# Index keys turned through four banks, new keys turned amid later blocks, finer waits, and another opening with the sample rows as 128 rows of 128

## The chip, the cores and the metric

The kernel runs on one core of one Trainium2 chip. The metric is the device time of one execution in microseconds (us), as the median of several executions. TensorE is called PE, VectorE DVE, ScalarE ACT, GpSimd POOL (Pool) and SyncE SP. "The profiled execution" is one more execution, recorded by the hardware profiler.

## The reference, cut to what matters

One decoder layer for 512 prompt tokens and 8 sample tokens (one per sequence), all in float32, `D_MODEL` 2048:

```python
h = x * rsqrt(mean(x*x) + 1e-6) * g            # RMSNorm of 512 + 8 rows
z = h @ w_in                                   # 2048 x 8848, columns split into
# q_r k_r v_r g_r | q_a k_a v_a g_a | q_i (16 heads x 128) k_i (128) w_i (16)
# retention: chunks of 128 tokens, per-head norm, gate silu(g_r)
# sparse attention: score = sum_h w_i * relu(q_i . k_i); top 128 of the prompt,
#   top 256 of 4097 for a sample (its 4096 old index keys lie in pages of
#   cache_kidx); softmax over the chosen keys; gate silu(g_a)
x = x + concat(ret, att) @ w_out
y = rmsnorm(x, final_norm_g)
```

Outputs are `y`, the new keys, values and index keys, and the retention states.

## The kernel before, in words

Each engine runs its own instruction list, written out in order by hand; semaphores join them. `X.wait_ge(s, n)` holds engine X until semaphore s has reached n, and everything behind it on that engine waits too.

**Blocks of the projection.** The weights are taken in 43 blocks of 256 columns (`chunk(n, a)`: block n, half a of the 2048 rows). SP loads a half into `Wraw` (`weights`), ACT copies it to a rounded high part `Wh` (`hi`), Pool subtracts to get the low part `Wl` (`lo`), and PE multiplies three times (Wh x Hh, Wh x Hl, Wl x Hh: lines 1448 to 1450) into PSUM banks 0 to 3. ACT empties the banks (`evacuate`, counted by `acc_free`). Block 0 is the index keys and index weights alone, blocks 1 to 8 the index queries (`q_i`), 9 and 10 the new keys and values (`kaT`, `vaT`), 11 to 18 attention queries and gates, 19 to 34 the retention heads (two blocks a head, h = (n - 19) / 2), 35 to 42 the output projection.

**The opening.** Five x tiles arrive in the order 0, 1, samples, 2, 3 (`ARRIVAL`). The sample tile has 8 rows of 2048. ACT takes the sums of squares (`squares`), DVE the inverse root (`norms`, `rsqrt`: two integer operations and three Newton steps of three operations) and scales the rows by it and by the gain (`scale`, L1016), PE turns each tile in four groups through banks 4 to 7 (`turn_tokens`), ACT copies a group to `Hh` (`high`), DVE subtracts to `Hl` (`low`, L1025). Then PE multiplies block 0 (`index_keys`, `index_weights`). `keep_busy` is turns of the identity whose result nobody reads.

**The index scores.** After block 8, PE makes 48 products `q_i . k_i` in banks 4 to 7, ACT takes relu into banks 1 and 2 in turn, DVE adds them up with the weights (L1083, `si_acc`) into `bm`.

**The old index keys.** Pool gathers 32 tiles `kx` of 512 KB into nine buffers (L870). PE turns them in 64 steps u (`turn_keys(u)`, four turns each) through three banks (3, 4, 5, by u % 3), ACT copies each step to one of six slots of `kT` (`keys_out(u)`, L650), and after every four steps, a group G, PE makes four products with the sample queries (`products(G)`, L1587), ACT a relu (`relu_group`, L658), and every second group PE two row products (`row_product`, L1596). Turn u waits for copy u - 3; copy u (from 6 on) waits for `products((u - 6) // 4)`. The first copy waits until DVE has added all 48 (`si_acc`), because of an `act.wait_ge(si_acc, n_si)`.

**The new keys and values** are turned (20 turns) after block 10 and copied to `kan` and `van` for storing and for attention.

**Retention head h = HP = 2.** Pool issues 16 small indirect DMAs (`candidate_rows`, `rowf`, L894), eight ahead of `rotary(h, 0)` and eight behind `rotary(h, 1)`; between the two lies `lo(n + 1, 1)`, the low part for block 24's second half.

**Before the output projection** DVE does `stats(7)` (the last head's norm), `keep_states_out(7)`, `samples_low` (low part of the sample columns, counted by `ms_lo`), `mix_low`, and the norm of the sample outputs (`gs_n`). PE's block 35 needs `ms_lo` for its third part and `gs_n` ahead of its second half.

Of the kernel before, what the change touches and what calls it, by code (L numbers as in the profile page):

```python
# [37 lines left out]
P = 128  # L38
# [39 lines left out]
def build(nc, x_prompt, x_sample, cache_k, cache_v, cache_kidx, state_ret, page_table, norm_g, w_in,  # L78
# [3 lines left out]
    with ctx:  # L82
# [56 lines left out]
        ptb, o = place("ptb", [P, NS, PAGES], I32, o)  # L139
        scores, o = place("scores", [NS * SEC, SKEY + 4], F32, 0)  # L140
# [13 lines left out]
        kT = mix[:, 0:6, 0:T]  # L154
# [68 lines left out]
        def turned_tile(v, r):  # L223

            return bank[4 + v % 4][:, :].rearrange("p (k t) -> p k t", k=4)[:, :, 0:r]
# [3 lines left out]
        x_in = [sem(f"x_in{i}") for i in range(5)]  # L229
        x_sq = sem("x_sq"); st4_set = sem("st4_set"); g_tr = sem("g_tr"); g_row = sem("gain_row_in"); ones_set = sem("ones_set"); g_mm = sem("gain_rows_mm"); x_norm = sem("x_norm"); x_tr = sem("x_tr")  # L230
# [32 lines left out]

        wiv = w_in[0].rearrange("(k p) c -> p k c", p=P)
# [74 lines left out]
        def _(sp):  # L339
# [30 lines left out]
            sp.wait_ge(x_in[2], 16)  # L370
            weights(0, 0)
            weights(0, 1)
# [98 lines left out]
        def _(act):  # L471
# [93 lines left out]
            def squares(i, c):  # L565

                act.wait_ge(x_in[i], 16)
                r = rows(i)
                if i == QT:
                    act.wait_ge(st4_set, 1)  # L570
                if c:
                    act.wait_ge(x_sq, c)
                nc.scalar.activation(junk[0:r, :], XT[0:r, i, :], ACT.Square,
                                     accum_out=st4[0:r, c:c + 1]).then_inc(x_sq, 1)

            def high(pos, which=range(4)):

                i = ARRIVAL[pos]
                for g in which:
                    v = 4 * pos + g  # L580
                    act.wait_ge(x_tr, v + 1)
                    nc.scalar.activation(Hh[:, 4 * g:4 * g + 4, tok(i)], turned_tile(v, rows(i)),
                                         ACT.Copy).then_inc(h_hi, 1)

            for pos, i in enumerate(ARRIVAL):
                src = x_prompt[0, P * i:P * i + P, :] if i < QT else x_sample.rearrange("b o m -> (b o) m")
                act.dma_start(XT[0:rows(i), i, :], src).then_inc(x_in[i], 16)
            act.dma_start(ptb[:, :, :].rearrange("p b j -> p (b j)"),
                          page_table.rearrange("b j -> (b j)").partition_broadcast(P)).then_inc(s_ptab, 16)
            for c, i in enumerate(ARRIVAL):  # L590
                squares(i, c)
# [3 lines left out]
            high(1)  # L595
            high(2)
            high(3)
            high(4)
# [28 lines left out]
            for t in range(1, QT):  # L627
                for h in range(NIH):
                    w = P * (t + 1)
                    act.wait_ge(si_mm, i + 1)  # L630
                    if i >= 2:
                        act.wait_ge(si_acc, i - 1)
                    nc.scalar.activation(bank[1 + i % 2][:, 0:w], bank[4 + i % 4][:, 0:w], ACT.Relu).then_inc(si_relu, 1)
                    i += 1
            n_si = i
# [8 lines left out]
            act.wait_ge(si_acc, n_si)  # L644

            def keys_out(u):
                act.wait_ge(kx_tr, u + 1)
                if u >= 6:
                    act.wait_ge(kq_mm, (u - 6) // 4 + 1)
                nc.scalar.activation(kT[:, u % 6, :], bank[3 + u % 3][:, :], ACT.Copy).then_inc(kt_ev, 1)  # L650
# [30 lines left out]
            for n in (9, 10):  # L681
                hi(n + 1, 0)
                if n == 9:
                    act.wait_ge(sc_out, 3)
                evacuate(n)
                hi(n + 1, 1)
            for m in range(4):
                dst = kan if m < 2 else van
                c = slice(P * (m % 2), P * (m % 2) + P)
                act.wait_ge(kv_tr, 2 * m + 1)  # L690
                nc.scalar.activation(dst[:, 0:QT, c], bank[4 + m % 2][:, :].rearrange("p (t d) -> p t d", t=QT),
                                     ACT.Copy).then_inc(kv_ev, 1)
                act.wait_ge(kv_tr, 2 * m + 2)
                nc.scalar.activation(dst[0:NS, QT, c], bank[6 + m % 2][0:NS, 0:P], ACT.Copy).then_inc(kv_ev, 1)
# [20 lines left out]
            for n in range(11, 19):  # L715
                hi(n + 1, 0)
                attention(2 * n)
# [119 lines left out]
        def _(pool):  # L837
# [12 lines left out]

            pool.wait_ge(g_mm, 4)
# [69 lines left out]
            for h in range(NH):  # L921
# [54 lines left out]
        def _(dve):  # L976
# [10 lines left out]
            def rsqrt(x, done=None):  # L987
# [3 lines left out]
                link(v_.tensor_scalar(y.bitcast(I32), x.bitcast(I32), 1, None, ALU.arith_shift_right))  # L991
                link(v_.tensor_scalar(y.bitcast(I32), y.bitcast(I32), -1.0, float(0x5f3759df), ALU.mult, ALU.add))
# [10 lines left out]
            def norms(a, b):  # L1003

                s = st4[:, a:b]
                dve.wait_ge(x_sq, b)
                link(v_.tensor_scalar(s, s, 1.0 / DM, EPS, ALU.mult, ALU.add))
                rsqrt(s)

            def column(i):  # L1010

# [924 lines left out]
```

## Time and profile before

| | |
|---|---|
| median of 3 runs | 1217.83 us (1217.45 to 1219.92) |
| the profiled execution: its time / its span | 1220.82 us / 1219.0 us |
| PE busy | 1176.8 us, 97% of the span |
| DVE, ACT, POOL busy | 51%, 37%, 47% |
| mean granted TensorE clock | 0.99 |
| chain that ended last | PE 91%, DVE 4%, ACT 2%, DMA 1% |

The span is from the first to the last instruction; 1.8 us lie around it. Busy time of an engine is a mean over stages, so with PE at 97% the question for each stage is where its 42 us without work lie and which engine ended each of those waits.

### The profile page before, as it was taken

How to read it: one execution, taken by the hardware profiler on the slowest of the kernel's cores; microseconds unless marked ns; L12 is line 12 of the kernel's file. 1: busy time of each engine (PE TensorE's matmuls, PEld its weight loads, DVE VectorE, ACT ScalarE, POOL GpSimd, SP SyncE). 2: the span in 40 equal slices, each digit the busy share in tenths (PEclk: the TensorE clock that was granted, in tenths of full speed). 3: DMA queues.
4: the chain of work that ended last, by engine and by line, in shares of the span. 5: the costliest groups of instructions: out<-in, count | busy, mean ns of one | idle time of the engine just before them, and what ended most of it. 6: DMA issues, size and time to landing. Idle time of an engine off the chain costs nothing.

```text
span 1219.0 us, 21955 instructions
## 1 busy us (share of the span) xinstructions
PE 1176.8 (97%) x9172; PEld 1110.3 (91%) x9172; DVE 620.0 (51%) x1199; ACT 452.1 (37%) x791; POOL 570.6 (47%) x262
## 2 busy tenths in 40 slices
PE   7999999899999999999999989999999999999995
PEld 5999995456999999999999979999999999999995
DVE  6500005998996994899998305343442544010013
ACT  5322225664223333333424323342524253232332
POOL 1355545240434333333635485846666384546450
PEclk9999999999999999999999999999999999999998
DMA  7233346380242222222343316446353525432213
GB/s 271 77 113 118 123 126 235 116 266 17 75 134 70 70 84 93 70 70 70 87 113 99 107 35 176 113 116 165 101 154 88 141 70 200 134 103 78 94 35 140
DMA packets 152840, 138.58 MB, mean 114 GB/s; under 512 B 4653, under 2 KB 145053, under 8 KB 151069
## 3 DMA queue, kind: packets, MB, share of 16 engines
q1 hardware_dynamic: 144502, 110.72, 30.5%
q0 software_dynamic: 6976, 22.03, 5.5%
q10 hardware_dynamic: 1280, 4.66, 1.0%
q8 instruction: 61, 1.00, 0.3%
q14 instruction: 21, 0.17, 0.0%
HBM read 127.02 MB, written 10.34 MB: 113 GB/s over the span
## 4 chain that ended last, share of the span: by engine, by line
PE 91%; DVE 4%; ACT 2%; issue 1%; DMA 1%; another core or an unknown queue 1%; DVEq 0%; ACTq 0%
PE bank L1448 25%; PE bank L1449 25%; PE bank L1450 25%; PE bank L1466 6%; PE bank L1559 2%; PE bank L1670 1%; PE bank L1652 1%; DVE bm L1083 1%; PE bank L1587 1%; DVE XT L1016 1%; PE bank L1825 1%; ACT mix L650 1%; DMA XT<-in_x_prompt 1%; PE bank L1596 1%
## 5 line engine op out<-in xcount | busy, mean ns | idle before, releaser
L1448 PE MATMUL bank<-Hh,Wh 128*128 128x264 f32 (+2 forms) x2432 | 711.8, 293 | 2.7 <-DVE Hl L1288 2.1
L1449 PE MATMUL bank<-Hl,Wh 128*128 128x264 f32 (+2 forms) x2432 | 703.4, 289 | 0.4 <-issue 0.4
L1450 PE MATMUL bank<-Hh,Wl 128*128 128x264 f32 (+2 forms) x2432 | 702.2, 289 | 0.5 <-issue 0.4
L842 POOL TENSOR_TENSOR Wl<-Wraw,Wh 128x2048 fp32r<-128x2048 f32 x84 | 386.8, 4606 | 477.3 <-ACT Wh L489 476.9
L1448 PEld LDWEIGHTS bank<-Hh,Wh 128*128 128x128 f32 x2432 | 459.7, 189 | 7.3 <-issue 6.4
L1449 PEld LDWEIGHTS bank<-Hl,Wh 128*128 128x128 f32 x2432 | 459.6, 189 | 3.1 <-issue 2.7
L1450 PEld LDWEIGHTS bank<-Hh,Wl 128*128 128x128 f32 x2432 | 458.7, 189 | 1.5 <-issue 1.5
L489 ACT ACTIVATE Wh<-Wraw 128x2048 fp32r<-128x2048 f32 x84 | 160.5, 1912 | 362.5 <-PE bank L1450 362.3
L1387 DVE TENSOR_TENSOR Y<-Y,bank 128x512 f32 (+1 forms) x16 | 10.4, 685 | 163.1 <-PE bank L1466 163.1
L1066 DVE COPY QS<-mix 128x128 f32<-128x128 f32 x1 | 0.3, 281 | 140.4 <-ACT mix L495 140.4
L870 POOL DMA_INDIRECT kx<-in_cache_kidx,pidx x32 | 30.4, 950 | 45.2 <-PE bank L1466 38.0
L1466 PEld LDWEIGHTS bank<-ident,kx 128*128 128x128 f32 x256 | 27.1, 141 | 23.8 <-issue 21.1
L900 POOL TENSOR_TENSOR XS<-XS,rot 128x520 f32<-128x520 f32 x16 | 21.2, 1322 | 44.6 <-ACT XW L547 44.6
L1466 PE MATMUL bank<-ident,kx 128*128 128x128 f32 x256 | 34.9, 279 | 7.0 <-ACT mix L650 4.7
L650 ACT ACTIVATE mix<-bank 128x512 f32<-128x512 f32 x64 | 34.9, 609 | 18.0 <-PE bank L1587 10.1
L1113 DVE MAX8 best<-scores 32x8 f32<-32x1025 f32 x32 | 38.9, 1217 | 5.1 <-ACT scores L677 4.1
L1145 DVE MAX8 top<-cand 8x8 f32<-8x1024 f32 x32 | 38.9, 1215 | 1.0
L1115 DVE FIND_INDEX8 besti<-best,scores 32x8 uint32<-32x1025 f32 x32 | 38.6, 1207 | 0.0
L1147 DVE FIND_INDEX8 besti<-top,cand 8x8 uint32<-8x1024 f32 x32 | 38.6, 1205 | 0.0
L1149 DVE MATCH_REPLACE8 cand<-top,cand 8x1024 f32<-8x1024 f32 x32 | 38.3, 1197 | 0.0
L1117 DVE MATCH_REPLACE8 scores<-best,scores 32x1025 f32<-32x1025 f32 x31 | 37.2, 1199 | 0.0
L1559 PE MATMUL bank<-kiT,mix 128*128 128x256 f32 (+2 forms) x96 | 33.8, 504 | 2.2 <-issue 1.4
(258 smaller groups left out, 1226.9 us busy)
## 6 DMA issues: line engine op xcount, KB each, us to landing
Wraw<-in_w_in SPq DMA_DIRECT2D x36, 1024.0 KB
Wraw<-in_w_in SPq DMA_DIRECT2D x64, 512.0 KB
Wraw<-in_w_out SPq DMA_DIRECT2D x16, 1024.0 KB
XT<-in_x_prompt ACTq DMA_DIRECT2D x4, 1024.0 KB, 9.0
sp__98<-in_state_ret SPq DMA_DIRECT2D x8, 512.0 KB, 4.0
out<-sp__98 SPq DMA_DIRECT2D x8, 512.0 KB, 5.1
Y<-in_x_prompt SPq DMA_DIRECT2D x1, 4096.0 KB
out<-Y SPq DMA_DIRECT2D x4, 1024.0 KB
```

The lines of the kernel that those rows point to most:

```text
L489: nc.scalar.activation(Wh[:, a, :, :], Wraw[:, a, :, :], ACT.Copy).then_inc(w_hi, 1)
L650: nc.scalar.activation(kT[:, u % 6, :], bank[3 + u % 3][:, :], ACT.Copy).then_inc(kt_ev, 1)
L842: nc.gpsimd.tensor_tensor(Wl[:, a, :, :], Wraw[:, a, :, :], Wh[:, a, :, :].bitcast(F32), ALU.subtract).then_inc(w_lo, 1)
L1113: link(v_.max(top, row))
L1115: link(v_.max_index(besti[:, 8 * (k // 3):8 * (k // 3) + 8], top, row))
L1145: link(v_.max(top, cand[:, :]))
L1147: link(v_.max_index(besti[0:NS, 8 * (k // 3):8 * (k // 3) + 8], top, cand[:, :]))
L1448: mm(bank[i][:, 0:w], wh, Hh[:, kk, s], start=(a == 0 and k == 0), stop=False)
L1449: mm(bank[i][:, 0:w], wh, Hl[:, kk, s], start=False, stop=False)
L1450: last = mm(bank[i][:, 0:w], wl, Hh[:, kk, s], start=False, stop=(a == 1 and k == KC - 1))
L1466: return nc.tensor.transpose(out, in_, ident[0:k, 0:k])
L1559: mm(bank[4 + i % 4][:, 0:w], mix[:, h, tok(t)], kiT[:, 0:w], start=True, stop=True).then_inc(si_mm, 1)
```

## The change

Seven edits; the diff below is cut to their core.

1. The sample rows are loaded as 128 rows of 128 (row 8k + b is piece k of sample b), their squares summed by one matmul with a 0/1 matrix `same`, scaled with gains `gs0` of that shape, and turned in one step instead of 16.
2. The inverse roots of tiles 0 and 2 move from DVE to Pool (`norm_root`: 14 chained operations on one column); the two integer operations of DVE's `rsqrt` become one, everywhere. The loads change order: the first weights are issued by ACT between tile 2 and tile 3, the page table by SP. Tile 1 is turned through banks 0 to 3. The fillers are 16 and 8 turns with the `same` matmul between them and 8 behind tile 0; the 8 ahead of `index_keys` go. `index_weights` of the first half stands ahead of tile 3's turns.
3. The index scores start at `acc_free` 32, with finer waits for the last two heads.
4. Old index keys: four banks (3, 4, 5, 2) and eight slots; the first turns wait for their own bank, the first copies for `qs_ready`.
5. The new keys are turned after the first half of block 10, the new values after the first half of block 11.
6. Two of the second eight `candidate_rows` move ahead of `lo(n + 1, 1)`.
7. `samples_low` stands ahead of `stats(7)`.

```diff
+        KB = (3, 4, 5, 2)
+        TURN_BANK = (4, 5, 6, 7, 0, 1, 2, 3, 4, 5, 6, 7, 4, 5, 6, 7, 4)
 # SP
+            sp.dma_start(gs0[:, :], ...to_broadcast([KT, NS, P])).then_inc(gs_in, 16)
-            sp.wait_ge(x_in[2], 16)
-            weights(0, 0)
-            weights(0, 1)
+            sp.wait_ge(x_in[3], 16)
+            sp.dma_start(ptb...)
 # ACT, opening
-            for c, i in enumerate(ARRIVAL): squares(i, c)
-            high(0) hi(0, 0) hi(0, 1) high(1) high(2) high(3) high(4)
+            rows_in(0) rows_in(1)  xs0 <- x_sample  rows_in(2)
+            first_weights(0) first_weights(1) rows_in(3)
+            squares(0, 0) squares(1, 1) squares(QT, 2) squares(2, 3)
+            high(0) hi(0, 0) hi(0, 1) high(1) high(QT) squares(3, 4) high(2) high(3)
 # ACT, keys
-            act.wait_ge(si_acc, n_si)
+            act.wait_ge(qs_ready, 1)
             def keys_out(u):
                 act.wait_ge(kx_tr, u + 1)
-                if u >= 6:
-                    act.wait_ge(kq_mm, (u - 6) // 4 + 1)
-                nc.scalar.activation(kT[:, u % 6, :], bank[3 + u % 3][:, :], ...)
+                if u >= 8:
+                    act.wait_ge(kq_mm, (u - 8) // 4 + 1)
+                nc.scalar.activation(kT[:, u % 8, :], bank[KB[u % 4]][:, :], ...)
 # Pool
+            def norm_root(a, b):      # every operation waits for the one before
+                link(g_.tensor_scalar(x, x, 1.0 / DM, EPS, ALU.mult, ALU.add))
+                link(g_.tensor_scalar(y..., x..., -0.5, float(0x5f3759df), ...))
+                for step in range(3):
+                    link(tensor_tensor) link(tensor_tensor) link(tensor_scalar)
+                    ins = g_.tensor_tensor(y if step < 2 else x, z, y, ALU.mult)
+            pool.wait_ge(x_sq, 1)
+            norm_root(0, 1)
+            pool.wait_ge(x_sq, 4)
+            norm_root(3, 4)
             pool.wait_ge(g_mm, 4)      # then the low parts of block 0
@@
                 rotary(h, 0)
+                if h == HP:
+                    candidate_rows(range(NS, NS + 2))
                 lo(n + 1, 1)
                 rotary(h, 1)
                 if h == HP:
-                    candidate_rows(range(NS, 2 * NS))
+                    candidate_rows(range(NS + 2, 2 * NS))
 # DVE
-                link(v_.tensor_scalar(y, x, 1, None, ALU.arith_shift_right))
-                link(v_.tensor_scalar(y, y, -1.0, float(0x5f3759df), ...))
+                link(v_.tensor_scalar(y, x, -0.5, float(0x5f3759df), ...))
-            norms(0, 2) scale(0) scale(1) norms(2, 5) low(0) low(1) scale(QT)
-            scale(2) low(2) scale(3) low(3) low(4)
+            (after the gb copies) scale(0, 1)          # waits rstd 1, from Pool
+            (mean of tile 1; wait sum_mm; mean of samples) rsqrt(st4[:, 1:3])
+            scale(1, 0) scale(QT, 0) low(0) low(1) low(QT)
+            scale(2, 2) rsqrt(st4[:, 4:5]) scale(3, 0) low(2) low(3)
@@
+            samples_low(KC, 1)
             stats(NH - 1)
             keep_states_out(NH - 1)
-            samples_low(KC, 1)
 # PE, opening
-            keep_busy(24, 6)
-            turn_tokens(0)
-            turn_tokens(1)
-            keep_busy(8, 3)
+            keep_busy(16, 6)
+            (wait x_sq 3, gb_copied 4) mm(bank[3][:, 0:1], same, xs2[:, 0:1])
+            keep_busy(8, 6)
+            turn_tokens(0, 1)
+            keep_busy(8, 2)
+            turn_tokens(1, 2)
+            turn_tokens(QT, 3)
             pe.wait_ge(h_lo, 8)
             pe.wait_ge(w_lo, 1)
             index_keys(0, slice(0, CUT))
-            turn_tokens(2)
-            turn_tokens(3)
+            turn_tokens(2, 4)
             pe.wait_ge(w_lo, 2)
             index_keys(1, slice(0, CUT)).then_inc(acc_done, 1)
-            turn_tokens(4)
             index_weights(slice(P, CUT))
-            pe.wait_ge(h_lo, 20)
+            turn_tokens(3, 5)
+            pe.wait_ge(h_lo, 17)
 # PE, scores and keys
-            pe.wait_ge(acc_free, 36)
+            pe.wait_ge(acc_free, 32)
+                    if t == 1 and h >= NIH - 2:
+                        pe.wait_ge(acc_free, 36 - 2 * (NIH - 1 - h))
-            pe.wait_ge(si_relu, i)
-            pe.wait_ge(qs_ready, 1)
-                if u >= 3:
-                    pe.wait_ge(kt_ev, u - 2)
+                if u >= 4:
+                    pe.wait_ge(kt_ev, u - 3)
+                elif u == 3:
+                    pe.wait_ge(si_acc, i)
+                elif u:
+                    pe.wait_ge(si_relu, i - 4 + u)
-            pe.wait_ge(si_acc, i)          # behind the first four turns
+            pe.wait_ge(qs_ready, 1)
+            pe.wait_ge(si_relu, i)
 # PE, new keys and values
             chunk(10, 0)
+            turn_new(0)                    # waits acc_free 40
             chunk(10, 1)
-            pe.wait_ge(acc_free, 44)
-            (all 20 turns)
+            chunk(11, 0), turn_new(1)      # waits acc_free 44
```

ACT's copies of the new keys and values follow in the same way: `new_out(0)` behind `hi(11, 0)`, `new_out(1)` behind `hi(12, 0)`.

## Rows read from the trace of the kernel before

**Rows 1.** Waits of PE over the whole span: waiter <- releaser, us, times, longest

```profile
PE bank L1466 <- ACT mix L650: 4.7, 11, 0.7
PE bank L1466 <- DVE Hl L1025: 3.9, 2, 3.4
PE bank L1825 <- ACT vn L781: 3.6, 1, 3.6
...
PE bank L1466 <- ACT bank L633: 1.3, 1, 1.3
PE bank L1466 <- ACT kan L694: 1.1, 1, 1.1
...
PE bank L1466 <- ACT vaT L532: 0.5, 1, 0.5
```

**Rows 2.** Timeline of DVE in the opening: start, duration, instruction

```profile
11.66 0.17 DVE L991 TENSOR_SCALAR rsq<-st 128x2 int32<-128x2 int32 x1
...
13.83 4.62 DVE L1016 SCALAR_TENSOR_TENSOR XT<-XT,st,gb 128x2048 f32<-128x2048 f32 x2
...
20.73 3.28 DVE L1025 TENSOR_TENSOR Hl<-bank,Hh 128x512 fp32r<-128x512 f32 x5
...
37.10 2.48 DVE L1025 TENSOR_TENSOR Hl<-bank,Hh 128x512 fp32r<-128x512 f32 x4 [1.11 <-ACT Hh L582]
```

**Rows 3.** Timeline of PE in the opening

```profile
21.57 3.50 PE L1466 MATMUL bank<-ident,XT 128*128 128x128 f32 x16 [3.37 <-DVE Hl L1025]
...
26.49 0.38 PE L1504 MATMUL bank<-Hh,W0h 128*128 128x256 f32 x1 [0.55 <-DVE Hl L1025]
...
35.83 1.91 PE L1466 MATMUL bank<-ident,XT 128*128 128x128 f32 x16
```

**Rows 4.** PE by stretches: stretch, us, busy (instructions), granted clock, DMA share, GB/s

```profile
22.00:23.00 1.00, 1.00 (x7) 0.50 0.00 0
...
1015.00:1016.00 1.00, 1.00 (x6) 0.50 1.04 313
```

**Rows 5.** Groups of instructions on POOL, shapes apart: count, busy us, mean ns

```profile
L918 POOL TENSOR_TENSOR QZ<-XS,XW 128x8 f32<-128x8 f32 x8 | 1.7, 212 | 0.0
```

**Rows 6.** Timeline of PE in the stage of the old index keys

```profile
226.88 1.53 PE L1466 MATMUL bank<-ident,kx 128*128 128x128 f32 x12 [1.29 <-ACT bank L633]
...
230.66 1.07 PE L1587 MATMUL bank<-mix,QS 128*32 128x512 f32 x8
...
288.14 1.07 PE L1587 MATMUL bank<-mix,QS 128*32 128x512 f32 x8 [0.69 <-ACT mix L650]
```

**Rows 7.** Timeline of ACT in the same stage

```profile
227.89 3.05 ACT L650 ACTIVATE mix<-bank 128x512 f32<-128x512 f32 x6 [0.94 <-DVE bm L1083]
...
251.06 1.58 ACT L650 ACTIVATE mix<-bank 128x512 f32<-128x512 f32 x3 [1.51 <-PE bank L1466]
```

**Rows 8.** Stretch 228 to 292 of all engines: busy of PE, PEld, DVE, ACT, POOL first

```profile
228.00:292.00 64.00, 57.28 (x431) 31.45 (x430) 58.80 (x151) 42.65 (x82) 21.77 (x23) 1.00 0.57 190
```

**Rows 9.** Stretch 230 to 277 of PE, in which Pool gathers

```profile
230.00:277.00 47.00, 41.95 (x311) 1.00 0.77 258
```

**Rows 10.** Timeline of DVE where attention first needs it

```profile
377.74 1.02 DVE L1171 SCALAR_TENSOR_TENSOR pb<-bank,bm 128x512 f32<-128x512 f32 x2 [10.90 <-PE bank L1652]
```

**Rows 11.** Timeline of POOL in head h = 2

```profile
707.62 4.61 POOL L842 TENSOR_TENSOR Wl<-Wraw,Wh 128x2048 fp32r<-128x2048 f32 x1
...
726.78 4.54 POOL L842 TENSOR_TENSOR Wl<-Wraw,Wh 128x2048 fp32r<-128x2048 f32 x1
```

**Rows 12.** Timeline of PE in head h = 2, last turn ahead of block 24's second half

```profile
712.03 0.27 PE L1466 MATMUL bank<-ident,pads 128*72 128x128 f32 x1
```

**Rows 13.** Timeline of PE in block 35

```profile
1014.63 0.54 PE L1448 MATMUL bank<-Hh,Wh 128*128 128x264 f32 x1 [2.10 <-DVE Hl L1288]
...
1022.50 0.27 PE L1466 MATMUL bank<-ident,OSn 128*128 128x128 f32 x1
```

**Rows 14.** Timeline of DVE in block 35

```profile
1020.86 0.35 DVE L1367 TENSOR_SCALAR OSn<-OSn,mv,st 128x128 f32<-128x128 f32 x1
```

More of the change, by code:

```diff
@@ L585, in _ @@
[L585 to L591, printed above, removed]
+                if i == QT:
+                    nc.scalar.activation(junk[:, 0:P], xs0[:, :], ACT.Square, accum_out=xs2[:, 0:1]).then_inc(x_sq, 1)
+                else:
+                    nc.scalar.activation(junk[:, :], XT[:, i, :], ACT.Square,
+                                         accum_out=st4[:, c:c + 1]).then_inc(x_sq, 1)
@@ L592, in _ @@
+            rows_in(0)
+            rows_in(1)
+            act.dma_start(xs0[:, :], x_sample[:, 0, :].rearrange("b (k c) -> k b c", k=KT)).then_inc(x_in[QT], 16)
+            rows_in(2)
+            first_weights(0)
+            first_weights(1)
+            rows_in(3)
+            squares(0, 0)
+            squares(1, 1)
+            squares(QT, 2)
+            squares(2, 3)
             high(0)
@@ L595, in _ @@
             high(1)
+            high(QT)
+            squares(3, 4)
             high(2)
             high(3)
-            high(4)
             hi(1, 0)
@@ L678, in _, with new_out @@
                                  bias=cols[0:NS * SEC, 6, 0:1]).then_inc(sc_out, 1)
[L681 to L694, printed above, removed]
+            def new_out(which):
+                for m in (2 * which, 2 * which + 1):
+                    dst = (kan, van)[which]
+                    c = slice(P * (m % 2), P * (m % 2) + P)
+                    act.wait_ge(kv_tr, 2 * m + 1)
+                    nc.scalar.activation(dst[:, 0:QT, c], bank[4 + m % 2][:, :].rearrange("p (t d) -> p t d", t=QT),
+                                         ACT.Copy).then_inc(kv_ev, 1)
+                    act.wait_ge(kv_tr, 2 * m + 2)
+                    nc.scalar.activation(dst[0:NS, QT, c], bank[6 + m % 2][0:NS, 0:P], ACT.Copy).then_inc(kv_ev, 1)
+            hi(10, 0)
+            act.wait_ge(sc_out, 3)
+            evacuate(9)
+            hi(10, 1)
+            hi(11, 0)
+            new_out(0)
+            evacuate(10)
+            hi(11, 1)
             def exps(h):
@@ L1628, in _, with turn_new @@
             chunk(9, 1)
+            def turn_new(which):
+                pe.wait_ge(acc_free, 40 + 4 * which)
+                for m in (2 * which, 2 * which + 1):
+                    src = (kaT, vaT)[which][:, m % 2, :]
+                    if m >= 2:
+                        pe.wait_ge(kv_ev, 2 * m - 2)
+                    for t in range(QT):
+                        last = turn(bank[4 + m % 2][:, P * t:P * t + P], src[:, tok(t)])
+                    last.then_inc(kv_tr, 1)
+                    turn(bank[6 + m % 2][0:NS, 0:P], src[:, T:NT]).then_inc(kv_tr, 1)
             chunk(10, 0)
+            turn_new(0)
             chunk(10, 1)
[L1632 to L1640 removed]
             def query_key(h):
@@ L1676, in _ @@
                     chunk(n, a)
+                    if n == 11 and a == 0:
+                        turn_new(1)
                     beta = 2 * n + a
```

159 lines of the change are left out of this document (95 added, 64 removed).

## The prediction

> **What bounds the kernel now.** I read the page first: PE is busy for 97% of the span, so a change can save only PE's work, PE's waits, or the slow clock that follows a wait. This change removes almost no PE work. I therefore read PE's list of waits next, because each entry names a place and a releaser. The reader should see three kinds in it [rows 1]: waits in the ring of the old index keys (4.7 us on ACT's copies, L650, and 1.3 at its start, L633), single waits at handovers (3.9 in the opening, 3.6 in head 2, 1.1 and 0.5 at the new keys), and one of 2.1 in block 35 [rows 13]. The timeline of each place then tells what would be late next, and the stretches tell the granted clock there.
>
> After two of these waits PE ran at 0.50 of its clock, 1.2 GHz: in the opening after 3.37 us without work, and in block 35 after 2.1 us [rows 3, 4, 13]. So such a wait costs more than itself. For the price I take block 35's matmuls: 0.22 us apart at the low level and 0.12 at the high one, over 3.4 us, which is about 1.6 us lost.
>
> **The opening (edits 1 and 2).** The old order of DVE is roots, two scalings, roots, and then eight subtractions of 0.656 us, which let PE's `index_keys` start at 26.49 [rows 2, 3]. In the new order:
> - The small identity sums and the four gain copies go ahead of everything. The identity is in SBUF at about 9 us, so the copies end near 12.1 instead of 10.9.
> - Pool's first root starts when tile 0's squares are there, at about 7.9. A Pool operation on 8 columns takes 0.212 us [rows 5]; with 0.08 for the link I take 0.29, and 14 of them end at 12.0. The lower bound is 0.21 each, and the upper is open, because this trace has no chained small Pool operations.
> - So DVE scales tile 0 from 12.1 to 14.4. It then does two means and ten root operations at 0.2 (one is 0.17 with a gap of 0.03 [rows 2]), 2.4 us, to 16.8; tile 1 to 19.1; the samples 0.3 to 19.4; and eight subtractions, 5.25 us, to 24.7. `index_keys` starts at about 24.8, which is 1.7 us earlier. Pool's low parts of block 0, behind two roots, are ready by 22.
>
> PE then loses most of this gain. Between the sample turn (about 21.3) and 24.8 it has no work for 3.5 us, and the 8 fillers that stood there are gone. The row for the same length of wait shows the clock at 0.50 right behind it [rows 3, 4], so 24 matmuls at first go 0.22 apart, about 1.5 us lost. From 26.3 in warm time: `index_keys` to 29.3, tile 2's turns 2.0, `index_keys` 2.9, `index_weights` 1.9, so tile 3's turns start at 36.1 against 35.83 before. Before, the weights' 1.9 us covered the copies and subtractions of the last tile; now nothing does. From the start of the turns to the last subtraction is 3.75 us (35.83 to 37.10 + 2.48) [rows 2, 3], giving 39.85 against 39.58. From there PE alone sets the pace, and block 1's weights are there 3 us ahead. I count the opening as 0. The bounds are 1.5 us saved (clock stays high) and 2.5 us lost (slower Pool steps).
>
> The Trainium skill speaks against this edit (TensorE: Matmul & The Clock Gate, What's actually happening): "the default state is throttled, and activity releases the throttle", so taking fillers out of a pause costs. The trace agrees, with 0.50 after the pause of 3.37 us. By the rule alone the opening would be slower; by the rows it is even, since DVE arrives earlier.
>
> **The start of the scores (edit 3).** PE may start 0.8 us earlier, but ACT's first relu stands behind `hi(9, 1)`, and after it DVE's additions, 0.855 us apart at the end, set the pace. Worth nothing, neither way.
>
> **The old index keys (edit 4).** First the start. The first copy waited for the last addition, at 227.89 [rows 7]; PE started turning at 226.88. Now u = 0, 1, 2 are turned from 225.6, ACT copies from 227.0, and only u = 3 (bank 2) waits for the last addition. Four turns of 0.51 from 228.0 give `products(0)` at 230.05 instead of 230.66 [rows 6]: 0.6 us.
>
> Then the ring. From `products(0)` to `products(15)` it takes 57.5 us [rows 6], 7.66 for two groups. PE's work for two groups is 8 turns of 0.51 (12 instructions in 1.53), two products of 1.0 and two row products of 0.42, in all 6.9. Over 7.5 pairs that leaves 5.7 us; the stretch shows 6.7 us without PE work from 228 to 292 [rows 8]. The waits follow from the order of ACT: turn u needs copy u - 3, and copy 4G + 6 needs `products(G)`, so twice a pair PE stands for 0.35 to 0.7 us. With four banks and eight slots, copy 4G + 6 needs only `products(G - 1)`, and a turn's bank was copied three turns (1.5 us) before; those waits go. What stays is a late ACT: four times in this stage it starts 0.8 to 1.8 us late while Pool issues gathers [rows 7], and a fourth bank covers about half of such a delay. I take 4.7 of the 6 us. Bounds: 2.4 (half of the waits come back) and 6.2 (all gone). Together with the start: 5.3 us, between 3 and 7.
>
> What is late next? The gathers must deliver 2.1 MB in 6.9 us, 304 GB/s; they ran at 258 with a DMA share of 0.77 [rows 9], which scales to 335. Close, but enough. DVE is still choosing from `bm` until 290.3, so it gains nothing from scores that come at 289; it had 10.9 us of slack where attention first needs it [rows 10], and loses about 4 of that.
>
> **The new keys (edit 5).** PE's waits of 0.5 and 1.1 [rows 1] vanish: both sets of turns now have copies behind them that ended a half block earlier. The 20 turns stay. ACT's 3.4 us of copies fall into half blocks of 12 us in which it has over 5 us free, and SP's stores are reached before the weights behind them are due. 1.6 us, with bounds of 1.2 and 1.8.
>
> **Head 2 (edit 6).** Pool has no gap from 693.8 to 731.3, so moving two issues (2.5 us) does not shorten it. It does delay the low part that began at 707.62 by 2.5 us, to end at 714.7, and PE reaches block 24's second half at 712.3 [rows 11, 12]. So a new wait of 2.4 us appears there, with the low clock behind it (1.6). In exchange the old wait of 3.6 on `vn` [rows 1], which ended 1.4 us after Pool's last issue, shrinks, since Pool's last issue stays at 726.8 and PE gets there later. Block 25 needs the low part that ends at 731.3 [rows 11]; PE got there at 732.0. Net 0, with bounds of 1.5 either way.
>
> **Block 35 (edit 7).** `samples_low` now runs in DVE's idle 2 us ahead of `stats(7)`, so PE's wait of 2.1 us and the low clock behind it go, 3.7 us. But next PE waits for `gs_n`. Its turn stood at 1022.5; the DVE result it needs was there at 1021.15 [rows 13, 14] and comes only 0.45 us earlier (two root operations, one subtraction). PE arrives at about 1019.0 and waits 1.7 us. The turn comes at 1020.8: 1.7 us saved, 0.1 if this pause lowers the clock again, 2.5 at best.
>
> **The tail.** One root operation less on the last chain: 0.2 us.
>
> **Sum.** 0 + 0 + 5.3 + 1.6 + 0 + 1.7 + 0.2 = 8.8 us. The profiled execution took 1220.82 us, 1219.0 of it span; that makes 1212.0. It is 3.0 above the median of 1217.83 shown, so for the median I predict 1209.0 us.
>
> **The rivals.**
> - *The ring is bound elsewhere* (14%). If late copies or the gathers keep PE waiting, edit 4 gives 1 to 2 us instead of 5.3. For it: DMA share 0.77 already, and ACT's late starts. Against it: no PE wait in the list names a DMA. Time: about 1213.
> - *The clock decides* (10%). PE's new pauses (before `index_keys`, block 24, `gs_n`) each bring the low level and nothing is given back: -1.5, -1.6 and -1.6 against my terms, about 1213.5. The reverse (the clock holds everywhere, and the whole ring becomes PE's own pace) gives about 1205 (15%).
> - *Slower* (5%): Pool's chained roots. If one step costs x instead of 0.29 us, tile 0 is scaled 14(x - 0.29) later and the whole opening follows. To eat 8.8 us, x must be 0.92 us; slower by more than 0.2% starts at 1.09. At 1.2 us the time is 1221.6. Against it: the 0.212 us row [rows 5]. The Trainium skill names the reason why Pool's small operations are dear (GPSIMD Engine Reference, 3.1 Elementwise): two software hops for each instruction and a join of eight cores.
> - *The moves do nothing measurable* (5%): gains before 300 us are taken back where DVE's choosing or Pool's chain in head 2 is the clock of the kernel. About 1217. Against it: DVE's 10.9 us of slack, and head 2 follows PE's own turns.
>
> **How the numbers follow.** My own case has 51% and lies within 1206 to 1212. I hold 0.2%, 2.4 us, to be about what a measurement of this kernel can tell from no change. The range takes in the fast case, the ring and the clock: 1204.0 to 1214.5. Outside it lie the last two rivals and little more. Faster by over 0.2% (under 1215.4): 51 + 14 + 10 + 15, less 1 for their edges, and 0 of the last two, so 0.89. Within 0.2%: 0.07. Slower: 0.04.
>
> **What the profile of the changed kernel would show.** Right: `index_keys` starts near 24.8 and the last subtraction of the opening ends near 39.8; `products(0)` to `products(15)` takes 51 to 54 us; no waits of PE on `kan` or `vaT`; a new wait on `Wl` (L842) near 704 of the new time; and PE waits on L1367 instead of L1288 in block 35. Wrong: Pool steps over 0.4 us apart, PE waiting for `kx` by DMA, or a low clock behind new pauses in which I count none.

## The result, and the profile after

| | before | after |
|---|---|---|
| median on the chip | 1217.94 us (12 runs) | 1222.95 us (12 runs, 1217.93 to 1224.76) |
| profiled execution: time / span | 1220.82 / 1219.0 us | 1223.86 / 1222.1 us |

The ratio is 1.0029, with an interval of 1.0018 to 1.0040: the change makes the kernel slower by 0.29%. (This ratio is estimated over the executions of both kernels and is not the quotient of the two medians, which is 1.0041 here; the same holds for the ratios further down.) I had predicted 1209.0 us, and slower had 4%.

The page of the changed kernel, its first part (busy us, share of the span, instructions):

```profile
PE 1173.9 (96%) x9159; PEld 1110.6 (91%) x9159; DVE 626.6 (51%) x1185; ACT 448.7 (37%) x788; POOL 580.1 (47%) x290
```

PE has 2.9 us less to do than before and 6 us more in which it does nothing. So the waits must tell it. PE's waits over the whole span, in the form of [rows 1]:

```profile
PE bank L1533 <- DVE kg L1330: 5.2, 1, 5.2
PE bank L1579 <- DVE Hl L1082: 4.9, 2, 3.0
PE bank L1566 <- issue: 4.3, 1, 4.3
...
PE bank L1515 <- POOL Wl L879: 2.8, 1, 2.8
PE bank L1913 <- DVE vx L1394: 2.1, 1, 2.1
PE bank L1533 <- DVE OSn L1434: 2.0, 1, 2.0
PE bank L1533 <- DVE XT L1075: 1.7, 2, 1.3
PE bank L1533 <- ACT mix L680: 1.5, 3, 0.5
```

What the change was to remove is gone: the ring's 4.7 is 1.5, and no wait names `kan` or `vaT`. In their place stand single long ones that were not there: 4.3 at the sum matmul of the samples (L1566), 5.2 and 2.1 behind DVE in head 2. The next step is to cut both timelines at matmuls that both have. The lengths between them, in us:

| from the landmark before to | before | after | difference | predicted |
|---|---|---|---|---|
| first matmul of the scores | 190.17 | 195.60 | +5.4 | 0 |
| `products(0)` | 40.49 | 39.74 | -0.75 | -0.6 |
| `products(15)` | 57.48 | 52.45 | -5.0 | -4.7 |
| first attention matmul on `kaT` | 88.46 | 86.33 | -2.1 | -1.6 |
| head 1, first matmul of `vn` with `kn` | 293.63 | 293.64 | 0 | 0 |
| head 3, the same | 115.46 | 121.04 | +5.6 | 0 |
| head 7, the same | 217.27 | 217.24 | 0 | 0 |
| the end | 216.04 | 216.06 | 0 | -1.9 |

They add up to the spans, 1219.0 and 1222.1. Three terms came as forecast or a little better. Two places that I had counted at zero cost 11 us, and the last term, block 35, brought nothing. Each length is that of one profile. The first has a spread: with the same opening as in the changed kernel the scores start at 194.18 (e3), 194.67 (e4) and 195.60, so the loss there is 4 to 5.4 us.

**The opening.** ACT in the changed kernel; `ACTq` rows are its own DMA issues:

```profile
2.37 0.67 ACTq L603 DMA_DIRECT2D XT<-in_x_prompt  x1
3.06 4.03 ACTq L607 DMA_DIRECT2D Wraw<-in_w_in  x2
7.12 4.87 ACTq L603 DMA_DIRECT2D XT<-in_x_prompt  x1
12.02 1.28 ACT L592 ACT_TABLE_LOAD   x1 [12.02 <-issue]
13.31 1.91 ACT L592 ACTIVATE junk<-XT 128x2048 f32<-128x2048 f32 x1
```

An issue of one block of rows takes 0.67 us at first. The two weight loads (each 128 x 8 pieces of 576 bytes) take 4.03 us to issue, and the block of rows behind them 4.87. Only then is ACT free for the squares: 13.31, against 5.83 in the kernel before:

```profile
5.83 1.91 ACT L573 ACTIVATE junk<-XT 128x2048 f32<-128x2048 f32 x1 [0.78 <-DMA XT<-in_x_prompt]
```

DVE scales tile 0 at 19.29 (13.83 [rows 2]), and PE:

```profile
21.70 3.32 PE L1533 MATMUL bank<-ident,XT 128*128 128x128 f32 x16 [1.33 <-DVE XT L1075]
...
31.26 0.54 PE L1579 MATMUL bank<-Hh,W0h 128*128 128x256 f32 x1 [2.97 <-DVE Hl L1082]
```

`index_keys` starts at 31.26 where [rows 3] had 26.49. The low clock follows the pause, as forecast: the matmuls start 0.21 us apart (stretch, us, busy of the five engines, granted clock, DMA share, GB/s):

```profile
32.00:34.00 2.00, 2.00 (x12) 2.00 (x11) 2.00 (x1) 0.00 (x0) 2.00 (x2) 0.50 1.08 376
```

**Head 2.** DVE first, then Pool, in the same microseconds:

```profile
711.72 2.89 DVE L1388 TENSOR_TENSOR kst<-raws,kst 8x128 fp32r<-8x128 f32 x1 [14.15 <-ACT raws L800]
...
722.97 6.02 DVE L1394 TENSOR_TENSOR vx<-vst,eye 72x1024 fp32r<-72x1024 f32 x1
...
740.07 8.45 DVE L1330 COPY_PREDICATED kg<-isnew,nkb 128x256 f32<-128x256 int32 x4 [7.71 <-DMA kg<-in_cache_k,rowu]
```

```profile
707.39 4.55 POOL L879 TENSOR_TENSOR Wl<-Wraw,Wh 128x2048 fp32r<-128x2048 f32 x1
...
723.38 4.53 POOL L879 TENSOR_TENSOR Wl<-Wraw,Wh 128x2048 fp32r<-128x2048 f32 x1
...
738.33 4.57 POOL L879 TENSOR_TENSOR Wl<-Wraw,Wh 128x2048 fp32r<-128x2048 f32 x1
743.35 4.53 POOL L879 TENSOR_TENSOR Wl<-Wraw,Wh 128x2048 fp32r<-128x2048 f32 x1 [0.46 <-ACT Wh L508]
```

The same operations in the kernel before, DVE and then Pool:

```profile
723.47 1.22 DVE L1327 TENSOR_TENSOR vx<-vst,eye 72x1024 fp32r<-72x1024 f32 x1
...
741.73 4.21 DVE L1263 COPY_PREDICATED kg<-isnew,nkb 128x256 f32<-128x256 int32 x4 [7.70 <-DMA kg<-in_cache_k,rowu]
```

```profile
740.01 4.61 POOL L842 TENSOR_TENSOR Wl<-Wraw,Wh 128x2048 fp32r<-128x2048 f32 x1
746.88 4.59 POOL L842 TENSOR_TENSOR Wl<-Wraw,Wh 128x2048 fp32r<-128x2048 f32 x1 [2.27 <-ACT Wh L489]
```

Read the lists by their ends. In the changed kernel Pool's subtraction ends at 727.91 and `vx` at 728.99. Pool's next two end at 742.90 and 747.88, and the four copies into `kg` end at 748.5. In the kernel before `vx` took 1.22 us in all eight heads, and the copies met one subtraction only: it ended at 744.62 and they at 745.94, before the next one began. Each of these DVE operations stands until Pool's subtraction is over, and does its own work then. PE waits for both, and for the late `Wl` at 712.00 that the prediction had.

From head 1's landmark to head 3's PE stands for 12.0 us in the changed kernel and 5.2 in the kernel before, 6.8 more. In turn PE is busy for 1.2 us less (109.1 and 110.3), as the low clock lasts less: in the kernel before it was 0.50 from 728 to 734, behind the wait of 3.6 us on `vn`; in the changed kernel it was 1.00 behind the wait of 2.8 us and about 0.5 to 0.6 only from 748 to 752. That leaves the 5.6 us of the table.

### The profile page after: what moved, and what is told of

It reads as the page before. It is cut to its first block, busy times and chain, and to the rows that moved or that the text cites. A ratio compares the mean times of both kernels' runs of the same rounds, so it can differ in the third digit from the quotient of the medians.

```text
span 1222.1 us, 21941 instructions
## 1 busy us (share of the span) xinstructions
PE 1173.9 (96%) x9159; PEld 1110.6 (91%) x9159; DVE 626.6 (51%) x1185; ACT 448.7 (37%) x788; POOL 580.1 (47%) x290
## 4 chain that ended last, share of the span: by engine, by line
PE 87%; DVE 6%; POOL 2%; issue 2%; ACT 1%; ACTq 1%; DMA 0%; DVEq 0%; POOLq 0%
PE bank L1515 24%; PE bank L1516 24%; PE bank L1517 24%; PE bank L1533 6%; PE bank L1752 1%; PE bank L1734 1%; PE bank L1634 1%; DVE bm L1150 1%; PE bank L1664 1%; POOL rowf L957 1%; PE bank L1673 1%; DVE Hl L1082 1%; ACTq L603 1%; PE bank L1909 0%; DVE kg L1330 0%
## 5 line engine op out<-in xcount | busy, mean ns | idle before, releaser
L1533 PE MATMUL bank<-ident,kx 128*128 128x128 f32 x256 | 32.4, 277 | 2.3 <-ACT mix L680 1.5
```

The costliest lines, as they stand in the source:

```text
L1533: return nc.tensor.transpose(out, in_, ident[0:k, 0:k])
```

## The experiments

Ratios are to the kernel before on the same chip and in the same round, with their intervals. Rounds e and f ran on one chip and round g on another. The kernel before took 1218.68 us in round e and 1221.78 in round f, so between rounds ratios are compared, not medians.

| run | median us / before | ratio |
|---|---|---|
| e1 first weights issued by SP | 1214.75 / 1218.68 | 0.9966 (0.9951 to 0.9981) |
| e2 roots back on DVE | 1222.60 / 1218.68 | 1.0025 (1.0011 to 1.0038) |
| e3 candidate rows 8 and 8 | 1216.86 / 1218.68 | 0.9987 (0.9978 to 0.9996) |
| e4 Pool waits for `vx` | 1219.95 / 1218.68 | 1.0016 (1.0008 to 1.0025) |
| f1 e1 and e3 together | 1212.55 / 1221.78 | 0.9921 (0.9902 to 0.9940) |
| f2 f1, old order in block 35 | 1212.36 / 1221.78 | 0.9927 (0.9902 to 0.9952) |
| f3 kernel before with edit 4 alone | 1217.86 / 1221.78 | 0.9963 (0.9946 to 0.9980) |
| f4 e3, one load on ACT | 1215.10 / 1221.78 | 0.9941 (0.9920 to 0.9961) |
| g1 f2 with the old opening | 1210.46 / 1218.17 | 0.9940 (0.9925 to 0.9956) |
| g2 f1, the pause filled | 1209.18 / 1218.17 | 0.9929 (0.9915 to 0.9943) |
| g3 kernel before with edit 6 alone | 1224.99 / 1218.17 | 1.0042 (1.0026 to 1.0058) |
| g4 e1 and e4 together | 1212.15 / 1218.17 | 0.9947 (0.9929 to 0.9965) |

### The opening: e1, e2, f4

Theory A: ACT is held by its own issues. Theory B: Pool's chained roots are slow. (Theory C and its rival D, in the expectations of e3 and e4, concern head 2.)

```diff
 e1 (SP's queue; the same two lines are taken from ACT's)
+            sp.wait_ge(x_in[2], 16)
+            weights(0, 0)
+            weights(0, 1)
             sp.wait_ge(x_in[3], 16)
```

> The changed kernel with one thing undone: the first block's two weight loads are issued by SP behind x tile 2 again, not by ACT between tiles 2 and 3. Theory A (ACT is held by its own DMA issues: 4.03 and 4.87 us for the weights and the fourth tile, so its first square starts at 13.3 us instead of 5.8): ACT's issues are over before 4 us, the first square starts near 5.9, index_keys near 25 instead of 31.3, and the time falls by about 6 us, to about 0.999 of before. Theory B (Pool's two chained roots set the opening): the roots stay, so the time falls by under 2 us.

```profile
2.37 1.16 ACTq L606 DMA_DIRECT2D XT<-in_x_prompt  x2
3.55 1.28 ACT L595 ACT_TABLE_LOAD   x1 [3.55 <-issue]
5.79 1.91 ACT L595 ACTIVATE junk<-XT 128x2048 f32<-128x2048 f32 x1 [0.95 <-DMA XT<-in_x_prompt]
```

Without the weight loads the two last blocks of rows are issued in 1.16 us, and the squares start at 5.79. `index_keys` starts at 23.74, 7.5 us sooner than in the changed kernel and 2.8 sooner than in the kernel before. The scores start at 187.97, 7.6 sooner than after, and the rest of the kernel keeps that. The ratio, 0.9966, is lower than the 0.999 that I expected: Theory A holds, and the issues cost more than I had put on them.

```diff
 e2: Pool's norm_root(0, 1) and norm_root(3, 4) go; on DVE
-            scale(0, 1)
+            dve.wait_ge(x_sq, 1)
+            link(v_.tensor_scalar(st4[:, 0:1], st4[:, 0:1], 1.0 / DM, EPS, ALU.mult, ALU.add))
+            rsqrt(st4[:, 0:1])
+            scale(0, 0)
 ... (tile 2 in the same way, column 3)
```

> The changed kernel with the roots of tiles 0 and 2 taken back from Pool to DVE; ACT still issues the first weights. Theory A (ACT's issues): ACT's first square still starts at 13.3, and only the difference between a Pool root (4.1 us) and a DVE root (2.2 us) is gained, at most 2 us on index_keys' start. Theory B (Pool's roots): the opening shortens by 5 us or more, to about 1.000 of before.

```profile
17.14 2.35 DVE L1071 SCALAR_TENSOR_TENSOR XT<-XT,st,gb 128x2048 f32<-128x2048 f32 x1
```

Tile 0 is scaled 2.2 us sooner, and `index_keys` starts at 29.08, also 2.2 sooner. But the scores start at 195.38, as in the changed kernel (195.60), and the ratio is 1.0025 beside 1.0029. The clock took most of the gain back. The `index_keys` of the last tokens start 1.75 us sooner (44.29, 46.04 in the changed kernel), both behind a wait of 1.90 us on `Hl`; here the granted clock fell behind it, and there it did not. PE by stretches, e2 and then the changed kernel:

```profile
46.00:48.00 2.00, 2.00 (x11) 0.50 0.03 8
```

```profile
46.00:48.00 2.00, 1.96 (x16) 1.00 0.04 12
```

Theory B falls: it asked for 5 us or more. The roots cost at most about 2 us of the opening, and e1, which leaves them on Pool, gives back more than the 5.4.

```diff
 f4 (with candidate rows 8 and 8): ACT's queue
             first_weights(0)
-            first_weights(1)
 SP's queue
+            sp.wait_ge(x_in[2], 16)
+            weights(0, 1)
             sp.wait_ge(x_in[3], 16)
```

> Candidate rows 8 and 8 again, and of the two first weight loads one stays on ScalarE (ahead of the last block of rows) and the second is issued by SyncE behind the third block of rows. Theory: ScalarE is held by the issues in proportion to what stands in its queue, so about half of the 7.6 us of the opening comes back: first square near 9.5 us, ratio half way between the two runs, 0.996. Rival: the queue only holds the engine once it is full, and one load does not fill it: first square at 6 us, the time of the run with both mended. Second rival: one load is enough to fill it, first square near 13, ratio 0.9987 as with the split alone undone.

```profile
3.01 0.51 ACTq L609 DMA_DIRECT2D Wraw<-in_w_in  x1
3.55 3.52 ACTq L605 DMA_DIRECT2D XT<-in_x_prompt  x1
7.11 1.28 ACT L594 ACT_TABLE_LOAD   x1 [7.11 <-issue]
8.40 1.91 ACT L594 ACTIVATE junk<-XT 128x2048 f32<-128x2048 f32 x1
```

One weight load is issued in 0.51 us, and it is the issue behind it that takes 3.52. So ACT is free at 3.55 with no load, 7.11 with one and 12.02 with two: 3.6 us for the first, 4.9 for the second. The hold grows with what stands in the queue, as the theory had it (first square at 8.4, I had said 9.5). `index_keys` starts at 26.36, between 23.70 with none and 31.26 with two, and the ratio is 0.9941 where I had expected 0.996: more than half came back. What in the queue holds the issue, the number of pieces, their size or the rows of x still ahead of them, no run separates.

### Head 2: e3, e4, g3, g4

```diff
 e3
-                if h == HP:
-                    candidate_rows(range(NS, NS + 2))
                 lo(n + 1, 1)
                 rotary(h, 1)
                 if h == HP:
-                    candidate_rows(range(NS + 2, 2 * NS))
+                    candidate_rows(range(NS, 2 * NS))
```

> The changed kernel with the second eight candidate-row gathers together again behind rotary(h, 1). Theory C (two gathers fewer at the end let Pool's low part of block 25 start while DVE's vx operation runs; vx and the predicated copy then stand behind Pool's, 6.0 and 8.1 us instead of 1.2 and 3.2, and the low part of block 24's second half comes 2.5 us late): head 2 costs what it did before, vx takes 1.2 us, the wait of 2.8 us on Wl goes, and the time falls by about 5 us, to 1.000 of before. Rival D (head 2 lost its time because PE arrives there earlier than before, whatever the order): the time stays within 1.5 us of the changed kernel.

```profile
719.08 1.22 DVE L1392 TENSOR_TENSOR vx<-vst,eye 72x1024 fp32r<-72x1024 f32 x1
736.43 4.12 DVE L1328 COPY_PREDICATED kg<-isnew,nkb 128x256 f32<-128x256 int32 x4 [7.80 <-DMA kg<-in_cache_k,rowu]
```

`vx` is back at 1.22 us, and the copies, at 4.12, meet one subtraction, as in the kernel before. From head 1 to head 3 it takes 114.76 us, against 121.04 after and 115.46 before: the split is what costs.

```diff
 e4, ahead of Pool's low part of block 25 (and in g4, with e1's edit)
+                if h == HP + 1:
+                    pool.wait_ge(vx_ready, h)
                 lo(n, 0)
```

> The changed kernel with one wait added: Pool starts the low part of block 25 only when DVE's vx of head 2 is done. Theory C: vx takes 1.2 us instead of 6.0, PE's wait of 2.1 us on vx goes, though Pool is about 1 us later; the predicated copy may meet a low part still. Time 2 to 4 us less than the changed kernel. Rival D: a wait more can only cost, up to 1 us more.

```profile
721.43 1.22 DVE L1396 TENSOR_TENSOR vx<-vst,eye 72x1024 fp32r<-72x1024 f32 x1
```

Only Pool's start is moved, by a wait of 0.89 us, and `vx` falls from 6.02 to 1.22 us. That shows the mechanism for `vx`. In this profile the copies met one subtraction only (3.49 us), and the stretch took 113.73 us; but that execution took 1215.14 us, and the ten others 1218.79 to 1221.19. Against the changed kernel the guard alone brings 1.6 us by the ratios (1.0016 beside 1.0029, and the intervals overlap), where e3 brings 5.1.

```diff
 g3, in the kernel before (edit 6 alone)
                 rotary(h, 0)
+                if h == HP:
+                    candidate_rows(range(NS, NS + 2))
                 lo(n + 1, 1)
                 rotary(h, 1)
                 if h == HP:
-                    candidate_rows(range(NS, 2 * NS))
+                    candidate_rows(range(NS + 2, 2 * NS))
```

> The kernel before with edit 6 alone: the first two of the later candidate rows are fetched between the two parts of the rotation, the other six behind it. Theory: Pool's long subtractions shift, and VectorE's operations with two operands in SBUF (the copy into kg, vx) stand behind them, as in the changed kernel: the stretch from head 1's to head 3's first state matmul (670.23 to 785.69) grows from 115.5 to about 121 us, ratio 1.0046. Rival (the prediction's step): net 0, within 1.5 us, ratio 0.999 to 1.001. Second rival: the loss in the changed kernel came from where the gains in front had put the fetches, and here it is about half.

```profile
726.07 2.53 DVE L1325 TENSOR_TENSOR vst<-raws,vst 8x128 fp32r<-8x128 f32 x1 [10.96 <-ACT raws L778]
728.63 1.22 DVE L1329 TENSOR_TENSOR vx<-vst,eye 72x1024 fp32r<-72x1024 f32 x1
741.00 8.39 DVE L1265 COPY_PREDICATED kg<-isnew,nkb 128x256 f32<-128x256 int32 x4 [7.78 <-DMA kg<-in_cache_k,rowu]
```

Two issues moved by one place, in the kernel before, cost 0.42%: from head 1 to head 3 it takes 122.08 us. `vx` is clear here, but the small `vst` ahead of it stood beside the subtraction (2.53 us, 0.28 in the kernel before), and the copies into `kg` (8.39 us) met two. PE waits 5.2 us for the copies, 2.9 for `Wl` and 1.7 for a `vx` that starts late. The loss needs none of the other edits; the "about half" of my second rival falls.

> The changed kernel with the first weight loads on SyncE, the candidate rows as the change has them, and Pool waiting in head 2 for VectorE's vx before its low part of block 25. Theory: it keeps vx clear but not the copies into kg, so it stays behind the run with both parts mended (0.9921) by about 3 us in most executions: ratio 0.994 to 0.995. Rival: as the profile with this guard alone showed 113.7 us between head 1's and head 3's state matmuls against 116.7 with both mended, the split is worth keeping once guarded: ratio 0.990.

With e1's opening the guarded split comes to 0.9947, as expected of it, behind 0.9921 of f1; the intervals overlap.

### The ring, the two undone together, and block 35: f1, f2, f3

```diff
 f3, in the kernel before (ACT's copies, then PE's turns; the products read slot % 8)
-                if u >= 6:
-                    act.wait_ge(kq_mm, (u - 6) // 4 + 1)
+                if u >= 8:
+                    act.wait_ge(kq_mm, (u - 8) // 4 + 1)
...
-                if u >= 3:
-                    pe.wait_ge(kt_ev, u - 2)
+                if u >= 4:
+                    pe.wait_ge(kt_ev, u - 3)
+                elif u == 3:
+                    pe.wait_ge(si_acc, i)
```

> The kernel before with the four banks and eight key slots alone (turns of index keys through banks 3, 4, 5, 2; nothing else of the change). Theory: the key stage is 5.0 us shorter, as measured in the changed kernel (52.4 against 57.4 us), and nothing gives it back: span 1214.0, time near 1213.5, ratio 0.9959. Rival: the blocks behind take it back, since their fetches and Pool's work stand at other places against VectorE: ratio 0.998 or above.

`products(0)` to `products(15)` takes 52.96 us, and the first attention matmul comes at 371.59 instead of 376.60. Of that, 4.5 us are the ring (57.48 before) and 0.5 lie ahead of `products(0)`. The span is 5.1 us less (1213.9), and the ratio of 0.9963 says 4.5.

> The changed kernel with two of its parts undone: the two first weight loads are issued by SyncE behind the third block of token rows, as in the kernel before, and the candidate rows are fetched 8 and 8 again. Theory: the two losses are apart in time and add, 7.6 us in the opening (scores and key stage end at 279.56 in place of 287.79 in the profile with the loads on SyncE) and about 6 us in head 2. From the changed kernel's span of 1222.1 that is near 1208.7, a time near 1210.5, ratio to the kernel before 0.993 to 0.995. Rival: a gain in front is given back in head 2, because Pool and VectorE then meet elsewhere: ratio 0.996 to 0.998, no better than with the loads moved alone.

f1 is the changed kernel with the diffs of e1 and e3. The two losses add: by the ratios e1 brings 0.0063 and e3 0.0042, and f1 0.0108. The ratio of 0.9921 is a little better than expected: a version that beats both kernels. From head 1 to head 3 it takes 116.72 us.

```diff
 f2 = f1 with
-            samples_low(KC, 1)
             stats(NH - 1)
             keep_states_out(NH - 1)
+            samples_low(KC, 1)
```

> As the run with both parts mended, and the lower halves of the samples' mixture stand behind the last head's statistics again, as in the kernel before (edit 7 undone). Theory: in the changed kernel the turn in block 35 came 1.3 us sooner, but the granted clock fell to 0.50 behind it and the stretch ended no sooner, so the edit is worth nothing here: the same time as with both mended, within 0.7 us. Rival (the prediction's step): 1.7 us slower than with both mended. Second rival: the low clock that the edit brought costs more than it gives, 1 us faster without it.

The medians differ by 0.2 us, as expected of it. PE's waits of this stretch say why. In f2 it is one of 1.8 on `Hl` (L1354); in f1 and in the changed kernel that is gone and the next is as long:

```profile
1024.34 0.33 PE L1533 MATMUL bank<-ident,OSn 128*128 128x128 f32 x1 [1.99 <-DVE OSn L1434]
```

### The new opening, and its pause: g1, g2

g1 is f2 with squares, roots, scalings, turns and `xs0` as in the kernel before.

> The old opening (squares, roots, scalings and turns as in the kernel before) with the ring, the start of the scores, the new keys and the shorter root of the changed kernel; candidate rows 8 and 8, old order in block 35. It differs from the run with both parts mended and the old tail in the opening alone. Theory: with the loads back on SyncE the new opening gains what index_keys' earlier start shows, 26.5 to 23.7, less what the clock takes: 2 us; so here the ratio is 0.9945 and the span near 1212.5. Rival: the pause of 2.97 us before index_keys eats the whole of it (the prediction's zero): ratio 0.993, the same as with both mended.

```diff
 g2 = f1 with
             turn_tokens(QT, 3)
+            pe.wait_ge(h_lo, 2)
+            keep_busy(16, 5)
```

> Both parts mended, and 16 identity turns (fillers of PE, with no use of their results) in PE's pause between the turn of the samples and the first index_keys matmul. Theory: the pause of 2.97 us is what lowers the granted clock behind it; with PE busy in it the index_keys matmuls go 0.12 us apart from the start in place of 0.21 over the first fifteen, 1.3 us sooner at the end of index_keys: ratio 0.992 less 0.001. Rival: the clock is set by more than this pause, and index_keys starts in the low level all the same: no gain, and up to 0.4 us lost if the fillers run past the last subtraction.

PE by stretches, f1 and then g2:

```profile
24.00:26.00 2.00, 2.00 (x16) 2.00 (x15) 2.00 (x1) 0.00 (x0) 2.00 (x2) 0.78 0.94 318
26.00:28.00 2.00, 2.00 (x11) 2.00 (x11) 1.82 (x7) 0.00 (x0) 1.28 (x1) 0.50 0.58 196
```

```profile
24.00:26.00 2.00, 2.00 (x19) 2.00 (x19) 2.00 (x1) 0.14 (x2) 2.00 (x2) 1.00 0.91 274
26.00:28.00 2.00, 1.45 (x13) 1.24 (x12) 1.86 (x6) 0.00 (x0) 1.60 (x1) 1.00 0.68 239
```

`index_keys` starts at 23.7 in both. With the pause filled, the clock stays at 1.00 behind it, and the scores start at 187.26. In f1 they start at 189.60, but there the clock fell a second time, behind the later wait of 1.9 us (0.50 from 40 to 42); in e1, f2 and g4, with the same opening and no second fall, they start at 187.97, 188.11 and 188.14. So the filler is worth 0.7 to 0.9 us in the profiles. In the ratios neither can be told from its partner (0.9929 beside 0.9921; g1 0.9940 beside f2's 0.9927), and each pair was measured on two chips. The scores start between 188.70 and 190.17 in four profiles of the old opening (the kernel before, f3, g3, g1), and between 187.97 and 189.60 in four of the mended one. What the new opening is worth once it is mended, 1 us or so, stays below what these runs separate.

## Why the prediction was wrong

- **The opening, 0 predicted, +5.4.** The step that failed is "Pool's first root starts when tile 0's squares are there, at about 7.9". The new place of the weight loads stood in the list of the change, and I priced when they land, not what their issue holds up. ACT stood in its own issues until 12.02, the squares came 7.5 us late (e1, f4), and the root started at 15.40. Behind that start the plan was sound: a Pool step took 0.27 us (0.29 predicted; 15.40 to 18.96 for 14), and with e1's edit the root starts at 7.88 and `index_keys` at 23.7, where I had 24.8. The low clock behind the pause came as priced.
- **Start of the stage, ring, new keys.** -0.75 (-0.6), -5.0 (-4.7) and -2.1 (-1.6, bounds to 1.8); what the 0.3 beyond the bound is, no run separates. f3, with edit 4 alone, has 4.5 for the ring and 0.5 for its start. ACT still ends the last wait of the ring, as predicted, and no wait there names a transfer.
- **Head 2, 0 predicted (bounds 1.5), +5.6.** The failed step is "Net 0". Its own waits were right: the new one on `Wl` is 2.8 (2.4 predicted), that on `vn` shrank from 3.6 to 0.6. The low clock priced behind the first did not come in this profile (1.00 there); in g3's it did (0.51 from 714 to 716). What was missing is that Pool's moved subtractions hold DVE: 2.1 at `vx` and 5.2 at `kg` (e3, e4, g3). I asked when Pool's results are due, not who else stops while Pool works. The trace of before had it, in the copies into `kg` themselves (4.21 us for four at 741.73, where the shortest one took 0.43) and in a group that I did not weigh, an operation on 128 x 4 numbers with a mean of 3.4 us:

```profile
L1220 DVE TENSOR_SCALAR st<-mv,cols 128x4 f32<-128x4 f32 x8 | 27.5, 3434 | 0.3
```

- **Block 35, -1.7 predicted, 0.** The wait on `OSn` came as forecast, 2.0 us (1.7), and the turn 1.2 us sooner (18.30 us behind head 7's landmark, 19.54 before). The failed step is that I took the pause as harmless to the clock and kept its fall as the bound of 0.1. The clock fell to 0.50 at 1026 to 1028, and the rest took 197.8 us instead of 196.5. In f4 it did not fall and 0.3 to 0.4 us remained against f3, where it held as well. The wait was moved, not shortened. The 0.2 of the root is below what can be read.
- **The rivals.** The forecast for "slower" was Pool's roots at 0.92 us a step or more; a step took 0.27, and e2 refutes them as the cause. The rival that named "Pool's chain in head 2" had the right place, but gains taken back are not what happened there: the split itself costs (g3), and the price was too small.

The Trainium skill (SBUF — State Buffer, Who interferes with whom) says that a DVE instruction with two SBUF inputs contends with a GpSimd instruction that reads SBUF; of the two-port modes it says that whoever issues first gets the shared ports for the whole instruction and the other "fully blocks". The traces agree that one stands for the whole of the other: `vx` took 6.02 us beside a subtraction of 4.53 and 1.22 alone. On the order they do not plainly agree: `vx` was recorded as starting at 722.97, 0.41 us ahead of the subtraction at 723.38, and still it was `vx` that stood.

## What to carry to other kernels

Price the issue of a transfer on the engine that issues it, in the order of its queue, and not only its landing: a compute engine with issues ahead of its work is late by all of them (here ACT was free at 12.02 instead of 3.55). When a long operation of Pool is moved, list which DVE operations it will now lie beside, and look in the trace for small DVE operations with a long mean. A wait removed ahead of a result that is itself nearly late is only moved.

## What the runs showed of the hardware that I had not expected

- ACT's issues: 0.44 to 0.67 us each with little in the queue; 3.52 us behind one load of 1024 pieces, and 4.03 and 4.87 with two. The Trainium skill (Perfetto Trace Analysis, DMA Instruction — HWDGE) has the issuing sequencer occupied until all descriptors are generated. The rows agree in that ACT starts nothing during an issue, but not in which issue is long: the load of 1024 pieces itself took 0.51 us, and the hold fell on the block of rows behind it (f4). In e1 SP issues the same two loads in 1.03 us, at 11.69, and ACT's squares start at 5.79.
- Not every DVE operation stands beside Pool's subtraction. In the changed kernel `vx` and `kg` did, with two operands in SBUF, and so did the `tensor_scalar` on 128 x 4 (3.9 us, 0.23 alone). `kst`, with two operands too, stood beside the two operations of the rotation that follow the subtraction (2.89 us, 0.28 alone). The selection's maxima (1.22 us) took the same time beside it as without it, and a sum along a row of 128 x 512 took 0.68 beside it. Operations with an operand in PSUM took 0.69 us for 128 x 512 beside it (376.48) and at most 0.69 anywhere else in that group (L1238).
- It works the other way too. Two steps of Pool's second root stood beside DVE's scalings of 2.35 us, and ended just after them (21.64 and 26.16):

```profile
20.09 1.61 POOL L899 TENSOR_SCALAR st<-st 128x1 f32<-128x1 f32 x1 [0.93 <-ACT junk L592]
...
23.99 2.22 POOL L905 TENSOR_TENSOR xs<-xs 128x1 f32<-128x1 f32 x1
```

- A pause of 2 us lowered PE's granted clock to 0.5 in some executions and left it at 1.00 in others (f4, block 35, wait of 2.0). The wait of 1.9 us in the new opening did the same: the clock fell behind it in e2 and f1, and held in the changed kernel, e1 and f2. Which one happens stays open. It makes 1.5 us, so edits of that size cannot be judged by one profile.
- The changed kernel's own times spread over 7 us (1217.93 to 1224.76), and those of e1 (1210.65 to 1217.5) and g3 (1217.18 to 1226.3), which have the split too, by 7 and 9; e3's, without it, spread over 4. That the copies into `kg`, whose start is set by a fetch, miss one of Pool's subtractions in the shorter ones would explain it; it is argued from e4's profile, not shown.
